# One feed-forward's gate/up products by Strassen's scheme on a quarter of K, and a transpose by one wide instruction and transfers

## What is computed

```python
def swiglu(h, w_gate, w_up, w_down):
    return (jax.nn.silu(h @ w_gate) * (h @ w_up)) @ w_down

x = x + 0.5 * swiglu(rmsnorm(x, norm_ffn1[l]), w1_gate[l], w1_up[l], w1_down[l])
...
x = x + 0.5 * swiglu(rmsnorm(x, norm_ffn2[l]), w2_gate[l], w2_up[l], w2_down[l])
```

## Time and profile before

| | |
|---|---|
| median of the runs | 1738.09 us |
| profiled execution, span | 1736.5 us |
| TensorE busy | 1727.4 us, 99% |
| TensorE weight loads | 1433.8 us, 83% |
| VectorE busy | 1149.5 us, 66% |
| ScalarE busy | 788.1 us, 45% |
| GpSimd busy | 19.6 us, 1% |
| matmuls recorded | 7734 |
| data moved | 334.51 MB, 193 GB/s on average |

### The profile page before, as it was taken

One profiled execution on the slowest core, in us unless ns is written; L12 is line 12 of the kernel. 1 busy time (PEld: TensorE's weight loads), 2 busy tenths in 40 slices (PEclk: granted clock), 3 DMA queues, 4 the chain that ended last, 5 costly groups with the idle time before them and its releaser, 6 DMA issues.

```text
span 1736.5 us, 20290 instructions
## 1 busy us (share of the span) xinstructions
PE 1727.4 (99%) x7734; PEld 1433.8 (83%) x7734; DVE 1149.5 (66%) x1491; ACT 788.1 (45%) x907; POOL 19.6 (1%) x24
## 2 busy tenths in 40 slices
PE   9999999999999999999999999999999999999998
PEld 7888888888888888888888888888888888888886
DVE  7766666666665566587877886666666666654554
ACT  6544444444444444454554554444444444443443
POOL 0000000000000000000040000000000000000000
PEclk9999999999999999999999999999999999999999
DMA  8656555565555555666544566656566565655552
GB/s 292 205 193 192 193 192 193 191 193 193 193 197 193 193 193 193 216 203 193 169 156 159 194 194 194 194 193 193 193 193 193 193 193 193 209 203 194 194 194 97
DMA packets 174945, 334.51 MB, mean 193 GB/s; under 512 B 6136, under 2 KB 18352, under 8 KB 174768
## 3 DMA queue, kind: packets, MB, share of 16 engines
q1 hardware_dynamic: 172960, 332.51, 58.5%
q10 hardware_dynamic: 1936, 1.32, 0.2%
HBM read 331.71 MB, written 2.10 MB: 192 GB/s over the span
## 4 chain that ended last, share of the span: by engine, by line
PE 99%; DMA 0%; ACT 0%; SPq 0%; DVE 0%; issue 0%; ACTq 0%; DVEq 0%
PE banks L437 31%; PE banks L439 31%; PE banks L438 31%; PE banks L456 2%; PE banks L423 2%; PE banks L426 1%; DMA raw<-in_w_gate 0%; PE banks L577 0%; PE banks L601 0%; PE banks L589 0%; PE banks L623 0%; PE banks L621 0%; PE banks L619 0%; PE banks L603 0%; PE banks L517 0%; ACT w_hi L722 0%
## 5 line engine op out<-in xcount | busy, mean ns | idle before, releaser
L996 DVE TENSOR_TENSOR w_lo<-raw,w_hi 128x1024 fp32r<-128x1024 f32 x622 | 763.4, 1229 | 551.5 <-ACT w_hi L722 549.4
L722 ACT ACTIVATE w_hi<-raw 128x1024 fp32r<-128x1024 f32 x622 | 658.1, 1060 | 905.1 <-PE banks L439 875.9
L437 PE MATMUL banks<-w_hi,act 128*128 128x512 f32 x1536 | 598.3, 390 | 0.0
L439 PE MATMUL banks<-w_lo,act 128*128 128x512 f32 x1536 | 597.6, 389 | 0.0
L438 PE MATMUL banks<-w_hi,act 128*128 128x512 f32 x1536 | 597.5, 389 | 0.0
L438 PEld LDWEIGHTS banks<-w_hi,act 128*128 128x128 f32 x1536 | 288.3, 188 | 60.1
L439 PEld LDWEIGHTS banks<-w_lo,act 128*128 128x128 f32 x1536 | 288.3, 188 | 59.7
L437 PEld LDWEIGHTS banks<-w_hi,act 128*128 128x128 f32 x1536 | 288.3, 188 | 59.6
L437 PE MATMUL banks<-w_hi,h 128*128 128x512 f32 x832 | 323.8, 389 | 0.0
L439 PE MATMUL banks<-w_lo,h 128*128 128x512 f32 x832 | 323.7, 389 | 0.0
L438 PE MATMUL banks<-w_hi,h 128*128 128x512 f32 x832 | 323.7, 389 | 0.0
(11 more groups left out here) (135 smaller groups left out, 466.2 us busy)
## 6 DMA issues: line engine op xcount, KB each, us to landing
raw<-in_w_down SPq DMA_DIRECT2D x88, 1024.0 KB, 5.0
raw<-in_w_gate SPq DMA_DIRECT2D x84, 1024.0 KB, 5.1
raw<-in_w_up SPq DMA_DIRECT2D x84, 1024.0 KB, 5.2
raw<-in_w_in SPq DMA_DIRECT2D x32, 1024.0 KB, 5.5
raw<-in_w_out SPq DMA_DIRECT2D x16, 1024.0 KB, 5.0
raw<-in_w_up SPq DMA_DIRECT2D x8, 512.0 KB, 9.9
raw<-in_w_gate SPq DMA_DIRECT2D x7, 512.0 KB, 9.9
xr<-in_x SPq DMA_DIRECT2D x8, 256.0 KB, 9.0
```

Source lines behind the costliest of these rows:

```text
L437: pe.matmul(dst, operand[:, k, hi], w_hi[:, s, w], start=k == first, stop=False)
L439: mm = pe.matmul(dst, operand[:, k, hi], w_lo[:, s, w], start=False, stop=k == last)
L722: act_e.activation(w_hi[:, s, :], raw[:, (p // 2) % RAW_SLOTS, off:off + PIECE], ACT.Copy).then_inc(hi_ready, 1)
L996: dve.tensor_tensor(w_lo[:, s, :], raw[:, (p // 2) % RAW_SLOTS, off:off + PIECE], w_hi[:, s, :].bitcast(F32), ALU.subtract).then_inc(lo_re ...
```

## The change

In superblocks 1 to 8 of each feed-forward the K tiles 0 to 3 are taken as a 2x2 block product: tokens in two halves and K in two pairs of tiles on one side, K in two pairs and gate/up on the other. It is computed by the Strassen-Winograd scheme with 7 block products in place of 8. Four combinations of the activations (`forms`) are made once per feed-forward; four combinations of the weights (T1 to T4) are made per superblock on VectorE (`add_sum`); the products lie in PSUM banks 4 to 7 beside the gate and up banks and are combined by VectorE in `fold_v`, `fold_v_n`, `fold_gate` and, in the next superblock, `merge`. Such a superblock has 20 pieces: pieces 0 and 1 have 3 matmuls each, pieces 3, 5, 7, 9, 11 and 13 have 6, the twelve others 12. The Silu comes after the last piece. The loop holds two superblocks, whose `raw` slots are shifted by 2.

The transpose of a superblock's result is one instruction over 128 partitions x 1024 columns (`square_h`), which transposes each 32x32 square in its place in the partitions. The squares are then moved to their partitions by 16 transfers on SP (`exchange`), each of 32 partitions x 2 runs of 512 B. `round_h` waits for all 16. This holds for all superblocks of both feed-forwards. In a fast superblock SP issues the exchange after its last chunk, in the others and in `down` after chunk 6.

The core of the diff (counting by pieces in place of turns, which touches most waits, is left out):

```diff
+FAST_SBS = 8
+FAST_PIECES = 20
+GATE_PIECES = (GATE_SBS - FAST_SBS) * 2 * SB_PIECES + FAST_SBS * FAST_PIECES
+MID_FIRST = GATE_PIECES + ROW_PIECES
+B11_0, B11_1, B21, T1, T3, B22, T2, T4 = 0, 1, 3, 5, 7, 9, 11, 13
+GATE_AT = {2: 4, 4: 6, 6: 8, 8: 10, 10: 12, 12: 14}
+UP_AT = {14 + n: 4 + 2 * n for n in range(6)}
+SUMS = (T1, T3, T2, T4)
+S5, S7, S2, S12 = range(4)
+P1_BANK, N5_BANK, N7_BANK, R6_BANK = 4, 5, 6, 7
+FAST_SLOTS = (0, 1, 2, 3, 2, 3, 0, 1)
+FAST_CHUNK = {0: (0, 0), 1: (0, 1), 2: (2, 0), 3: (0, 2), 4: (2, 2), 6: (3, 0), 7: (1, 0), 8: (3, 2),
+              9: (1, 2), 10: (4, 0), 11: (1, 2), 12: (4, 2), 14: (5, 0), 15: (5, 2), 16: (6, 0),
+              17: (6, 2), 18: (7, 0), 19: (7, 2)}
+FAST_FREE = (-6, -4, -2, 0, 5, 9, 12, 12)
+COPY_P1_AT, ROUND_FAST_AT = 8, 17
+FOLD_AT = (15, 16, 17)
+MERGE_AT, PRODUCT_AT, SQUARE_H_AT, SPLIT_FAST_AT = 2, 4, 13, 18
...
+            def exchange(n, dst):
+                sp.wait_ge(h_squared, n + 1)
+                for q in range(SB):
+                    for c in range(SB):
+                        for_half = dst[c * SQ:(c + 1) * SQ, :, :, :].rearrange(
+                            "p (t q) k j -> p t q (k j)", q=SB)[:, :, q, :]
+                        sp.dma_start(for_half, squared[q * SQ:(q + 1) * SQ, c, :, :]
+                                     .rearrange("p (t k) j -> p t (k j)", k=SB)).then_inc(h_turned, 16)
...
+            def load_fast(f, i, shift):
+                first, fi = fast_first(f, i), f["sb"] + i
+                for c, (part, kc) in enumerate((("gate", 0), ("up", 0), ("gate", 1), ("gate", 2),
+                                                ("gate", 3), ("up", 1), ("up", 2), ("up", 3))):
+                    slot = (FAST_SLOTS[c] + shift) % RAW_SLOTS
+                    sp.wait_ge(lo_ready, first + FAST_FREE[c])
+                    sp.dma_start(raw[:, slot, :].rearrange("p (t n) -> p t n", n=QCOLS),
+                                 f[part][kc * 4 * P:(kc + 1) * 4 * P, bass.ds(i * QCOLS, QCOLS)]
+                                 .rearrange("(t p) n -> p t n", p=P)).then_inc(raw_landed[slot], 16)
+                exchange(fi - 1, turned)
...
+            def add_product(bank, hi, lo, s, j, first, last):
+                dst, w = banks[:, bank, :], slice(j * QCOLS, (j + 1) * QCOLS)
+                pe.matmul(dst, hi, w_hi[:, s, w], start=first, stop=False)
+                pe.matmul(dst, lo, w_hi[:, s, w], start=False, stop=False)
+                return pe.matmul(dst, hi, w_lo[:, s, w], start=False, stop=last)
+            def form_product(p, form, bank, first, last):
+                for j in range(2):
+                    mm = add_product(bank, forms[:, 0, form, j, :], forms[:, 1, form, j, :],
+                                     p % SPLIT_SLOTS, j, first and j == 0, last and j == 1)
+                return mm
+            def tile_product(p, j, k, t, bank, first, last):
+                return add_product(bank, act[:, k, t * P:(t + 1) * P],
+                                   act[:, k, S + t * P:S + (t + 1) * P], p % SPLIT_SLOTS, j,
+                                   first, last)
+            def fast_gate_up(f, i, shift):
+                first, fi = fast_first(f, i), f["sb"] + i
+                pe.wait_ge(silu_ready, fi)
+                for p in range(FAST_PIECES):
+                    pe.wait_ge(lo_ready, first + p + 1)
+                    if p in (B11_0, B11_1):
+                        mm = tile_product(p, 0, p, 0, P1_BANK, p == B11_0, p == B11_1)
+                    elif p in GATE_AT:
+                        k = GATE_AT[p]
+                        for t in range(2):
+                            mm = rows_of(t, p % SPLIT_SLOTS, GATE_BANK, act, (k, k + 1), 4,
+                                         (KT - 1, KT)[t])
+                    elif p in UP_AT:
+                        k = UP_AT[p]
+                        for t in range(2):
+                            mm = rows_of(t, p % SPLIT_SLOTS, UP_BANK, act, (k, k + 1),
+                                         (KT, 4)[t], KT - 1)
+                    elif p == B21:
+                        for j in range(2):
+                            mm = tile_product(p, j, 2 + j, 0, GATE_BANK, False, False)
+                    elif p == T1:
+                        pe.wait_ge(forms_ready, f["fast"] // FAST_SBS + 1)
+                        mm = form_product(p, S5, N5_BANK, True, True)
+                    elif p == T3:
+                        mm = form_product(p, S7, N7_BANK, True, True)
+                    elif p == B22:
+                        pe.wait_ge(product_ready, fi)
+                        mm = form_product(p, S12, UP_BANK, True, False)
+                    elif p == T2:
+                        mm = form_product(p, S2, R6_BANK, True, True)
+                    else:
+                        for j in range(2):
+                            mm = tile_product(p, j, 2 + j, 1, GATE_BANK + 1, False, j == 1)
+                    mm.then_inc(piece_used, 1)
...
+            def square_h(n):
 
                 dve.wait_ge(product_ready, n + 1)
-                ins = turn_squares(dst, gu, 2 * step, 2)
-                if step == TURN_STEPS - 1:
-                    ins.then_inc(h_turned, 1)
+                dve.transpose(squared[:, :, :, :].rearrange("p c m j -> p m c j"),
+                              gu[:, :, :].rearrange("p t (k c i) -> p (t k) c i", c=SB, i=SQ))\
+                   .then_inc(h_squared, 1)
...
+            def make_forms(f):
+                def form_stepped(ins):
+                    form_steps[0] += 1
+                    ins.then_inc(form_step, 1)
+                    dve.wait_ge(form_step, form_steps[0])
+                dve.wait_ge(act_ready, f["norm"] * KT + 4)
+                dve.tensor_tensor(whole[:, :, :, :], act[:, 0:4, 0:S].bitcast(F32)
+                                  .rearrange("p k (t n) -> p k t n", n=P),
+                                  act[:, 0:4, S:2 * S].bitcast(F32)
+                                  .rearrange("p k (t n) -> p k t n", n=P),
+                                  ALU.add).then_inc(whole_act_ready, 1)
+                dve.wait_ge(whole_act_ready, f["fast"] // FAST_SBS + 1)
+                a11, a21 = (whole[:, 0:2, t, :] for t in range(2))
+                a12, a22 = (whole[:, 2:4, t, :] for t in range(2))
+                s5, s7, s2, s12 = (raw_forms[:, n, :, :] for n in range(4))
+                form_stepped(dve.tensor_tensor(s5, a21, a22, ALU.subtract))
+                form_stepped(dve.tensor_tensor(s2, a11, s5, ALU.subtract))
+                dve.tensor_tensor(s7, a21, a11, ALU.subtract)
+                dve.tensor_tensor(s12, a12, s2, ALU.subtract).then_inc(raw_forms_ready, 1)
...
+            def split_forms(f):
+                n = f["fast"] // FAST_SBS + 1
+                dve.wait_ge(forms_hi_ready, n)
+                dve.wait_ge(raw_forms_ready, n)
+                dve.tensor_tensor(forms[:, 1, :, :, :], raw_forms[:, :, :, :],
+                                  forms[:, 0, :, :, :].bitcast(F32),
+                                  ALU.subtract).then_inc(forms_ready, 1)
+                dve.wait_ge(forms_ready, n)
+                dve.memset(folds[:, :, :], 0.0).then_inc(folded, 1)
...
+            def add_sum(nth, p, turn, shift):
+                low, high = slice(0, PIECE), slice(PIECE, 2 * PIECE)
+                gate, up = raw[:, FAST_SLOTS[0] + shift, :], raw[:, FAST_SLOTS[1] + shift, :]
+                if p == T1:
+                    for c in range(2):
+                        dve.wait_ge(raw_landed[FAST_SLOTS[c] + shift], (turn + 1) * 16)
+                    dst, a, b = sums[:, :], gate[:, low], up[:, low]
+                elif p == T3:
+                    dst, a, b = up[:, low], up[:, low], up[:, high]
+                elif p == T2:
+                    dve.wait_ge(summed, 4 * nth + 1)
+                    dst, a, b = up[:, high], sums[:, :], up[:, high]
+                else:
+                    dve.wait_ge(summed, 4 * nth + 3)
+                    dst, a, b = sums[:, :], up[:, high], gate[:, high]
+                dve.tensor_tensor(dst, a, b, ALU.add).then_inc(summed, 1)
...
+            def merge(first, merges):
+                dve.wait_ge(piece_used, first)
+                dve.wait_ge(folded, merges)
+                dve.tensor_tensor(folds[:, :, :], banks[:, UP_BANK:UP_BANK + 2, :], folds[:, :, :],
+                                  ALU.add).then_inc(merged, 1)
...
+            def fold_v(first, nth):
+                dve.wait_ge(piece_used, first + T2 + 1)
+                dve.wait_ge(p1_copied, nth + 1)
+                dve.tensor_tensor(folds[:, 0, :], banks[:, R6_BANK, :], folds[:, 1, :],
+                                  ALU.subtract).then_inc(fold_step, 1)
+            def fold_v_n(nth):
+                dve.wait_ge(fold_step, 3 * nth + 1)
+                dve.tensor_tensor(gu[:, 1, :], banks[:, N7_BANK, :], folds[:, 0, :], ALU.add)
```

(85 more changed lines are left out.)

228 lines of the change are left out of this document (152 added, 76 removed).

## The result

The changed kernel takes 1750.27 us (median of 4 runs, 1748.94 to 1750.84) against 1738.10 of the kernel before beside it (4 runs, 1737.96 to 1738.16): ratio 1.0069, interval 1.0057 to 1.0081. It is slower by 0.7%. The forecast was 1719.5 us; what happened is rival (a), its slower half. The profiled execution has a span of 1749.1 us.

A forecast was written before the change was run, and what follows sets the result against it. The prediction took TensorE's number of matmuls as the bound. Span 1736.5 less 21.8 saved plus 3.2 lost at the forms gave 1717.9, with 1.6 from span to median 1719.5 us; range 1715.5 to 1755.

The forecast's parts named there:

- rival (a): SP's queue: the exchange holds the loads back; 0.15 that some gain is left, 0.20 slower, 1808 us at the top.
- TensorE's part: Superblocks 1 to 8: 186 matmuls for 192, 42.16 us for 43.52, 21.8 us saved in all.
- p: Time per transfer of the exchange's 16 on SP's queue: between 0.42 and 0.95 us, taken as 0.49, 7.8 us together.
- Split 2': VectorE's split of piece 2 in the next superblock: ends at 34.8 + 16p us after TensorE began piece 0.
- 43.7: Latest time in us, from TensorE's start of piece 0, for the next superblock's piece 2 split before TensorE stalls.
- the cover: Spare time before TensorE waits for the next superblock's piece 2 split: 1.1 us, gone at p = 0.56.
- c0' and c1': The next superblock's first two chunks, behind the exchange on SP: predicted to land at 34.5 and 37.5 us.
- T 21.5: Predicted end of the wide transpose on VectorE, 21.5 us after TensorE began piece 0 of the superblock.
- VectorE's part: VectorE's work per fast superblock: 37.7 us of 42.16, 89%, where it was 29.4 of 43.52.
- Rival (b): VectorE becomes the bound if the wide transpose costs 7.0 us: about 1738 us, chance 0.06; slower, 0.03.
- The forms: VectorE's activation combinations, once per feed-forward: 3.2 us lost in the first, between 1 and 5; hidden in the second.
- Rival (c): The longer loop is fetched again at 6 back edges of about 1.8 us: 11 us, 1731 us, chance 0.04.

The follow-up runs named there:

- e1: Changed kernel with the wide transpose at piece 7 instead of 13 and the exchange issued after the sixth chunk of the same superblock: 1718.82 us, ratio 0.989.
- e8: Changed kernel's Strassen superblocks without wide transpose and exchange, 16 narrow transposes at pieces 6 to 13 instead: 1737.93 us, ratio 1.0.
- e4: Changed kernel without Strassen superblocks, all in the old loop, keeping the wide transpose and the exchange: 1738.18 us, ratio 1.0.
- e5: Changed kernel with only the wide transpose moved to piece 7 from 13, exchange still behind the last chunk: 1719.54 us, ratio 0.9893.
- e9: Kernel before, with six groups of 8 small transfers added after its last store; issue took 0.60 us from SBUF, 0.43 from HBM with 32 partitions.
- e3: Changed kernel with the 16 exchange transfers issued on GpSimd's queue instead of SP's: 1757.38 us, ratio 1.0113.
- e6: Changed kernel with the exchange cut into 32 transfers of half the size instead of 16: 1918.0 us, ratio 1.1036.

## Why the prediction was wrong

**TensorE's part: right.** 96 matmuls fewer; e1's span of 1716.7 us is 19.8 below's execution, close to the 21.8 saved less the 2.1 lost at the forms.

**The step that failed is p.** The rule was right, and I put a wrong number into it. "Split 2' ends at 34.8 + 16p" with the allowed 43.7 gave the break-even at p = 0.64. I took p = 0.49 from the issues at the kernel's start. All of those read HBM; the exchange reads SBUF:

```profile
L388 SPq DMA_DIRECT2D turned<-squared x320: 585/597/1407, 78.1 to 1476.2; - x160
```

```profile
L405 SPq DMA_DIRECT2D raw<-in_w_gate x64: 367/373/407, 33.7 to 1377.2; - x64
```

0.597 us recorded, 0.64 from start to start ((221.71 - 212.10)/15), and from the first of 16 to the next chunk's issue 222.97 - 212.10 = 10.87 us, which is p = 0.68. The formula then gives 34.8 + 10.9 - 43.7 = 2.0 us per superblock; 2.2 were measured. The lower end 0.42 for p was "the issue alone" of the wrong source, and "I take p = 0.49, since only one chunk is still in flight" weighed only the queue's backlog. I had named the missing row myself ("the patterns of these transfers occur nowhere in it") and still gave the forecast 0.52 and the slower end 0.20, with the cover gone at 0.56. An unknown with bounds 0.42 and 0.95, and a threshold at 0.56, doesn't bear such chances.

**The third chunk, and the 43.7.** I followed c0' and c1' and took c2' as landed. It is issued last of the three, lands 9.5 us after its issue and ends the ring. It costs little: split 2' waited 0.24 us for it (VectorE's row of 234.87), since the two sums and splits 0' and 1' end at 234.62 anyway. The 0.2 between 2.0 and 2.2 is a slip in the 43.7: TensorE asks for piece 2' a superblock and two short pieces after piece 0, at 42.16 + 1.36 = 43.52. With that the formula gives 2.15 us, and the cover was gone at p = 0.545; its smaller terms nearly cancel.

**The transpose's time.** Predicted T 21.5; with piece 0 at 189.83 it ended at 212.08, T 22.3. The 0.8 more is piece 2's own late start: from piece 2 (191.87) it is 20.2 us, and 21.5 - 1.36 = 20.1 was predicted.

**VectorE's part: too high, on the safe side.** Predicted 37.7 us per fast superblock, 89%; e1 shows 83%, 35.0 us. The wide transpose was 1.238 us (taken 1.23), the merge 1.218 (1.3), the folds 0.68 (0.682), the memset 0.91 (1.1). What I missed is that back-to-back instructions overlap: the sums at 231.06 and 232.20 start 1.14 us apart with 1.23 recorded, and the earlier trace rows had three splits in 3.50 us. Rival (b) is refuted by the transpose's duration. It holds in another form: without the wide transpose TensorE waits for VectorE (e8).

**The forms.** Predicted 3.2 us in the first feed-forward; piece 0 of the first fast superblock comes 1.6 us late, after the memset, and piece 2 a little more:

```profile
53.65 1.07 PE L542 MATMUL banks<-w_hi,act 128*128 128x512 f32 x4
56.16 0.50 PE L625 MATMUL banks<-w_hi,act 128*128 128x512 f32 x1 [1.44 <-DVE w_lo L1427]
...
57.42 0.39 PE L627 MATMUL banks<-w_lo,act 128*128 128x512 f32 x1
57.89 0.50 PE L523 MATMUL banks<-w_hi,act 128*128 128x512 f32 x1
```

56.16 less 53.65 + 4 x 0.2267 is 1.6; 57.89 less 57.65 is 0.24; with two slow first matmuls it is 2.1. TensorE was kept waiting nowhere earlier: the 0.4 us that I put on split 14 isn't there. In the second feed-forward nothing is lost at the forms, as predicted.

**The account.** 1736.5 - 21.8 = 1714.7. Measured 1749.1, 34.4 more: 31.0 in 14 fast superblocks, 2.1 at the first; superblock 0 itself ended 0.9 later than before (54.56 against 53.65), which e1, ending it at 53.25, has not, so I put it on the start of the run. 0.4 is left without a place.

**The other steps.** The exchange in superblocks 9, 10 and `down` costs nothing, as said (e4). The last of the 16 transfers landed 1.9 us after its issue, some 12 us after the first one's issue: the landing is paid once, the issue 16 times. The reading of the Trainium skill's rule on small transfers ("DMA: Bandwidth & Descriptors", Rules for kernel authors) by which each would pay its fixed part in turn, 29 us, is refuted by that number. Rival (c): between 100 and 394 us two packets each on two instruction queues appear, where the earlier trace rows has none; e1 has the same loops and the same packets, and TensorE does not stop in that stretch.

Open: why SBUF as a source takes 0.17 us more per issue; whether an exchange of fewer, larger transfers would do, which wasn't tried.

## What to carry to other kernels

Before putting transfers ahead of loads on an in-order queue, follow every load behind them to the matmul that needs it, and price the issues by rows with the same source. Where the price lies near the break-even, start the chain earlier: here moving one VectorE instruction by six pieces turned +0.7% into -1.1% (e5). Two halves that each give nothing alone (fewer matmuls, less VectorE) can give the gain together, so test the pair.

## What the runs showed of the hardware

An SP issue with SBUF as source took 0.60 us (0.62 for 128 partitions), from HBM 0.43 to 0.47 for the same small patterns (e9) and 0.37 for 1 MB chunks (the changed kernel); on GpSimd's queue 16 of them took 8.4 us, 0.53 each (e3). Transfers of 32 KB landed after 1.9 us with only their own kind under way (e9), and after 5.4 on GpSimd's queue beside 1 MB loads (e3). A 128x1024 float32 transpose took 1.24 us, an addition of that size 1.22, and a 32x256 transpose 0.44. After TensorE had idled 9.4 us its next 12 matmuls ran at a granted clock of 0.50, the 107 after them at 1.00 (e6). After waits of 1.5 to 3.1 us the clock of the next 4 us was 1.00 in 14 of 16 cases, and 0.66 and 0.59 in two (e3); the changed kernel's waits, up to 1.7 us, left the stretches from 100 to 394 and from 1083 to 1394 us at 1.00.
